# Two attention heads at a time through TensorE, in different halves of its rows and columns

## What is computed

```python
def softmax_with_sink(logits, sink):
    sink_col = jnp.broadcast_to(sink, logits.shape[:-1] + (1,))
    p = jax.nn.softmax(jnp.concatenate([logits, sink_col], axis=-1), axis=-1)
    return p[..., :-1]
...
    s_band = jnp.einsum('bkgnqd,bknsd->bkgnqs', qb, kb).astype(jnp.float32) * scale
    s_band = jnp.where(valid, s_band, NEG_INF)
    s_ctx = jnp.einsum('bkgnqd,bksd->bkgnqs', qb, kc).astype(jnp.float32) * scale
    p = softmax_with_sink(jnp.concatenate([s_band, s_ctx], axis=-1), sink_b).astype(v.dtype)
    o = (jnp.einsum('bkgnqs,bknsd->bkgnqd', p[..., :3 * BLOCK], vb)
         + jnp.einsum('bkgnqs,bksd->bkgnqd', p[..., 3 * BLOCK:], vc))
```

## Time and profile before

| | |
|---|---|
| median of three runs | 2931.18 us (2930.18 to 2934.03) |
| profiled execution | 2938.37 us, its span 2936.5 us |
| TensorE busy | 2618.6 us, 89% of the span |
| VectorE busy | 1804.7 us, 61% |
| ScalarE busy | 1053.3 us, 36% |
| chain that ended last | TensorE 50%, VectorE 15%, DMA 7%, ScalarE 6% of the span |

### The profile page before, as it was taken

One profiled execution on the slowest core, in us unless ns is written; L12 is line 12 of the kernel. 1 busy time (PEld: TensorE's weight loads), 2 busy tenths in 40 slices (PEclk: granted clock), 3 DMA queues, 4 the chain that ended last, 5 costly groups with the idle time before them and its releaser, 6 DMA issues.

```text
span 2936.5 us, 34811 instructions
## 1 busy us (share of the span) xinstructions
PE 2618.6 (89%) x13100; PEld 1942.9 (66%) x13100; DVE 1804.7 (61%) x3315; ACT 1053.3 (36%) x1930; POOL 443.0 (15%) x575
## 2 busy tenths in 40 slices
PE   6899997999997997899987999999789999698997
PEld 2788885645886996333443888887377777357776
DVE  2775786556656786234557556555578872555895
ACT  2222222223223343210332222223347862244784
POOL 1011110100001110002000433443012210100220
PEclk9899998999998998897997999999889999797999
DMA  6566662422244785110101000000159982004896
GB/s 245 168 200 201 208 190 71 167 72 72 74 164 156 250 289 165 36 63 24 36 22 36 1 1 1 1 1 1 58 199 353 339 312 79 15 8 131 303 335 220
DMA packets 115047, 386.72 MB, mean 132 GB/s; under 512 B 20160, under 2 KB 22336, under 8 KB 114624
## 3 DMA queue, kind: packets, MB, share of 16 engines
q1 hardware_dynamic: 76640, 276.33, 27.6%
q0 software_dynamic: 34848, 95.47, 10.1%
q10 hardware_dynamic: 3392, 12.70, 1.1%
HBM read 389.66 MB, written 26.21 MB: 142 GB/s over the span
## 4 chain that ended last, share of the span: by engine, by line
PE 50%; DVE 15%; DMA 7%; ACT 6%; issue 2%; POOL 1%; DVEq 0%; ACTq 0%; SPq 0%; POOLq 0%
PE ps L143 49%; DMA RG<-in_w 6%; DVE moe0wl L152 2%; DVE moe1wl L152 2%; DVE acc L160 1%; PE ps L146 1%; ACT moe0wh L149 1%; DMA AR<-in_a 1%; DVE rwMM L172 1%; ACT moe1wh L149 1%; DVE rwa L152 1%; DVE H L160 1%; ACT L149 1%; POOL rwML L152 0%; DVE X L160 0%
## 5 line engine op out<-in xcount | busy, mean ns | idle before, releaser
L143 PE MATMUL ps<-H,RG 128*128 128x256 f32 (+2 forms) x1088 | 365.8, 494 | 15.1 <-ACT H L149 15.1
L160 DVE SCALAR_TENSOR_TENSOR acc<-AR,cs,acc 128x512 f32<-128x512 f32 x420 | 296.4, 747 | 45.4 <-DMA AR<-in_a 43.3
L143 PEld LDWEIGHTS ps<-H,RG 128*128 128x128 f32 (+1 forms) x1088 | 209.2, 195 | 160.8 <-issue 135.0
L152 DVE TENSOR_TENSOR moe0wl<-RG,moe0wh 128x1024 fp32r<-128x1024 f32 x144 | 173.7, 1222 | 39.7 <-ACT moe0wh L149 36.1
L199 POOL DMA_DIRECT2D AR<-in_a x152 | 81.6, 537 | 695.2 <-DVE acc L160 534.4
L149 ACT ACTIVATE moe0wh<-RG 128x1024 fp32r<-128x1024 f32 x144 | 152.1, 1062 | 73.4 <-DMA RG<-in_w 37.3
L152 DVE TENSOR_TENSOR moe1wl<-RG,moe1wh 128x1024 fp32r<-128x1024 f32 x120 | 144.4, 1222 | 29.3 <-ACT moe1wh L149 26.6
L152 DVE TENSOR_TENSOR rwXX<-rwXX,ps 128x512 f32<-128x512 f32 x144 | 92.6, 643 | 111.2 <-PE ps L143 111.2
L149 ACT ACTIVATE f1wh<-RG 128x1024 fp32r<-128x1024 f32 x66 | 70.0, 1062 | 230.7 <-PE ps L143 230.5
L143 PE MATMUL ps<-f1hh,f1wh 128*128 128x512 f32 x352 | 142.8, 406 | 8.6 <-DVE f1hl L152 8.6
L149 ACT ACTIVATE moe1wh<-RG 128x1024 fp32r<-128x1024 f32 x120 | 126.3, 1061 | 56.3 <-DMA RG<-in_w 29.1
(11 more groups left out here) (634 smaller groups left out, 6295.1 us busy)
## 6 DMA issues: line engine op xcount, KB each, us to landing
RG<-in_w SPq DMA_DIRECT2D x525, 512.0 KB, 4.8
AR<-in_a POOLq DMA_DIRECT2D x152, 512.0 KB, 3.9
moe0back<-moe_outs ACTq DMA_DIRECT2D x4, 1024.0 KB, 8.0
CT<-in_consts ACTq DMA_DIRECT2D x1, 2546.0 KB, 18.4
X<-in_x ACTq DMA_DIRECT2D x1, 2048.0 KB, 11.5
moe_rows<-moe0ht POOLq DMA_DIRECT2D x4, 512.0 KB, 5.0
moe1back<-moe_outs ACTq DMA_DIRECT2D x2, 1024.0 KB, 5.8
X<-in_ctx ACTq DMA_DIRECT2D x1, 1024.0 KB, 7.0
```

The lines of the kernel that those rows point to most:

```text
L143: return Silent() if self.e is None else self.e.matmul(out, lhs, rhs, start=start, stop=stop, skip_group_check=True)
L152: return Silent() if self.e is None else self.e.tensor_tensor(out, a, b, op)
L160: return Silent() if self.e is None else self.e.scalar_tensor_tensor(out=out, in0=a, scalar=s, in1=b, op0=op0, op1=op1)
```

## The change

`Attention` takes pairs of heads. In each round TensorE computes the scores of both heads, one after the other into two banks, and transposes the weights of both; VectorE and ScalarE do their steps for one head and then the other. The weighted sums of a pair go into one bank, head 0 in partitions 0 to 63 and head 1 in 64 to 127, with the products of the two alternating, and one copy of 128 partitions empties it. In m1 and GQA the two heads of a pair lie in partitions 0 to 63 and 64 to 127; in MLA both lie in partitions 0 to 95. Weighing comes one round behind instead of two, the turn two instead of three. There are 2 x 4 + 3 = 11 rounds in m1 instead of 20, and 19 in MLA and in GQA instead of 36. A round takes two steps of the modulation instead of one. m1's projections stand in rounds 2 to 9, MLA's in rounds 3, 5, to 15, with ScalarE one and VectorE two rounds behind. The ring of exponentials has 6 slots (3 rounds of 2), the turned weights are kept for 2 pairs.

```diff
-    LAG, RINGS = 3, 5
-
-    def __init__(self, g, st, S, name, ada, units, scale, dv):
-        self.g, self.S, self.name, self.ada, self.units, self.scale, self.dv = g, S, name, ada, units, scale, dv
+
+    LAG, RINGS = 2, 6
+
+    def __init__(self, g, st, S, name, ada, pairs, scale, dv):
+        self.g, self.S, self.name, self.ada, self.pairs, self.scale, self.dv = g, S, name, ada, pairs, scale, dv
         self.E = g.sb(st, name + "s", [P, self.RINGS, 512])
-        self.PT = g.sb(st, name + "pt", [P, 3, 4, 256])
+        self.PT = g.sb(st, name + "pt", [P, 2, 2, 4, 256])
         self.sm = g.sb(st, name + "sm", [P, self.RINGS, 8])
-        self.n = len(units)
+        self.n = len(pairs)
 
     def ready(self):
         return [self.S.dve.at(("o", self.n - 1))]
 
     def parts(self, u):
 
-        n2 = 2 * self.n
-        return (u if u < n2 else None, u - 2 if 2 <= u < n2 + 2 else None, u - self.LAG if self.LAG <= u < n2 + self.LAG else None,
-                (u - self.LAG - 2) // 2 if u >= self.LAG + 2 and (u - self.LAG) % 2 == 0 else None)
+        inside = lambda r: r if 0 <= r < 2 * self.n else None
+        pair = u - self.LAG - 2
+        return inside(u), inside(u - 1), inside(u - self.LAG), pair // 2 if pair >= 0 and pair % 2 == 0 else None
 
     def rounds(self):
         return range(2 * self.n + self.LAG + 1)
@@ -1382,32 +1383,42 @@
                 beside(e, u)
             now, weigh, turn, pair = self.parts(u)
             if now is not None:
-                q, k, nk, vs, out, mask, sink = self.units[now // 2]
-                h = now % 2
-                ps = g.banks.take((name, "s", now))
-                for tok in g.banks.free((name, "s", now)):
-                    e.wait_ge(*tok)
-                e.matmul(ps[:, 0:nk], q[:, h * P:(h + 1) * P], k, True, True).then_inc(*p.up(("s", now)))
-            self.ada.fill_pe(e, 1)
+                qs, ks, nk, vs, out, masks, sinks = self.pairs[now // 2]
+                h, got = now % 2, []
+                for s in range(2):
+                    got.append(g.banks.take((name, "s", now, s)))
+                    for tok in g.banks.free((name, "s", now, s)):
+                        e.wait_ge(*tok)
+                for s in range(2):
+                    e.matmul(got[s][:, 0:nk], qs[s][:, h * P:(h + 1) * P], ks[s], True, True).then_inc(*p.up(("s", now, s)))
+            self.ada.fill_pe(e, 2)
             if turn is not None:
-                nk = self.units[turn // 2][2]
-                ps = g.banks.take((name, "t", turn))
-                for tok in g.banks.free((name, "t", turn)):
-                    e.wait_ge(*tok)
-                e.wait_ge(*S.dve.at(("w", turn)))
-                for j in range(nk // P):
-                    ins = e.transpose(ps[:, j * P:(j + 1) * P], self.E[:, turn % self.RINGS, j * P:(j + 1) * P], g.C("ident"))
-                ins.then_inc(*p.up(("t", turn)))
+                nk = self.pairs[turn // 2][2]
+                for s in range(2):
+                    ps = g.banks.take((name, "t", turn, s))
+                    for tok in g.banks.free((name, "t", turn, s)):
+                        e.wait_ge(*tok)
+                    e.wait_ge(*S.dve.at(("w", turn, s)))
+                    for j in range(nk // P):
+                        ins = e.transpose(ps[:, j * P:(j + 1) * P], self.slot(turn, s)[:, j * P:(j + 1) * P], g.C("ident"))
+                    ins.then_inc(*p.up(("t", turn, s)))
             if pair is not None:
-                q, k, nk, vs, out, mask, sink = self.units[pair]
+                qs, ks, nk, vs, out, masks, sinks = self.pairs[pair]
                 ps = g.banks.take((name, "o", pair))
                 for tok in g.banks.free((name, "o", pair)):
                     e.wait_ge(*tok)
-                e.wait_ge(*S.act.at(("t", 2 * pair + 1)))
-                b = out.base_partition()
+                e.wait_ge(*S.act.at(("t", 2 * pair + 1, 1)))
                 for j in range(nk // P):
-                    ins = e.matmul(ps[b:b + self.dv, 0:256], vs[j], self.PT[:, pair % 3, j, :], j == 0, j == nk // P - 1)
+                    for s in range(2):
+                        ins = e.matmul(ps[s * self.dv:(s + 1) * self.dv, 0:256], vs[s][j], self.PT[:, pair % 2, s, j, :], j == 0,
+                                       j == nk // P - 1)
                 ins.then_inc(*p.up(("o", pair)))
+
+    def ring(self, r, s):
+        return (2 * r + s) % self.RINGS
+
+    def slot(self, r, s):
+        return self.E[:, self.ring(r, s), :]
 
...
-            if now is not None:
-                q, k, nk, vs, out, mask, sink = self.units[now // 2]
-                m, s = self.sm[:, now % self.RINGS, :], self.E[:, now % self.RINGS, 0:nk]
-                e.wait_ge(*S.dve.at(("m", now)))
-                if sink is not None:
-                    e.activation(m[:, 2:3], sink, ACT.Exp, bias=m[:, 1:2]).then_inc(*a.up())
-                src, sc = (s, 1.0) if mask is not None else (g.banks.of((name, "s", now))[:, 0:nk], self.scale)
-                e.activation(s, src, ACT.Exp, bias=m[:, 1:2], scale=sc, accum_out=m[:, 3:4]).then_inc(*a.up(("e", now)))
-                if mask is None:
-                    g.banks.done((name, "s", now), a.now())
-            if turn is not None:
-                nk, tp, h = self.units[turn // 2][2], turn // 2, turn % 2
-                e.wait_ge(*S.pe.at(("t", turn)))
-                if tp >= 3:
-                    e.wait_ge(*S.pe.at(("o", tp - 3)))
-                e.activation(self.PT[:, tp % 3, 0:nk // P, h * P:(h + 1) * P],
-                             g.banks.of((name, "t", turn))[:, 0:nk].rearrange("p (j n) -> p j n", n=P),
-                             ACT.Copy).then_inc(*a.up(("t", turn)))
-                g.banks.done((name, "t", turn), a.now())
+            for i in range(2) if now is not None else ():
+                qs, ks, nk, vs, out, masks, sinks = self.pairs[now // 2]
+                m, s = self.sm[:, self.ring(now, i), :], self.slot(now, i)[:, 0:nk]
+                e.wait_ge(*S.dve.at(("m", now, i)))
+                if sinks is not None:
+                    e.activation(m[:, 2:3], sinks[i], ACT.Exp, bias=m[:, 1:2]).then_inc(*a.up())
+                src, sc = (s, 1.0) if masks is not None else (g.banks.of((name, "s", now, i))[:, 0:nk], self.scale)
+                e.activation(s, src, ACT.Exp, bias=m[:, 1:2], scale=sc, accum_out=m[:, 3:4]).then_inc(*a.up(("e", now, i)))
+                if masks is None:
+                    g.banks.done((name, "s", now, i), a.now())
+            for i in range(2) if turn is not None else ():
+                nk, tp, h = self.pairs[turn // 2][2], turn // 2, turn % 2
+                e.wait_ge(*S.pe.at(("t", turn, i)))
+                if tp >= 2:
+                    e.wait_ge(*S.pe.at(("o", tp - 2)))
+                e.activation(self.PT[:, tp % 2, i, 0:nk // P, h * P:(h + 1) * P],
+                             g.banks.of((name, "t", turn, i))[:, 0:nk].rearrange("p (j n) -> p j n", n=P),
+                             ACT.Copy).then_inc(*a.up(("t", turn, i)))
+                g.banks.done((name, "t", turn, i), a.now())
 
...
-            if weigh is not None:
-                q, k, nk, vs, out, mask, sink = self.units[weigh // 2]
-                m, s = self.sm[:, weigh % self.RINGS, :], self.E[:, weigh % self.RINGS, 0:nk]
-                e.wait_ge(*S.act.at(("e", weigh)))
-                if sink is not None:
+            for i in range(2) if weigh is not None else ():
+                qs, ks, nk, vs, out, masks, sinks = self.pairs[weigh // 2]
+                m, s = self.sm[:, self.ring(weigh, i), :], self.slot(weigh, i)[:, 0:nk]
+                e.wait_ge(*S.act.at(("e", weigh, i)))
+                if sinks is not None:
                     e.tensor_tensor(m[:, 3:4], m[:, 3:4], m[:, 2:3], ADD).then_inc(*v.up())
                     e.wait_ge(*v.now())
                 e.reciprocal(m[:, 4:5], m[:, 3:4]).then_inc(*v.up())
                 e.wait_ge(*v.now())
-                e.tensor_scalar(s, s, m[:, 4:5], None, MUL).then_inc(*v.up(("w", weigh)))
-            if now is not None:
-                q, k, nk, vs, out, mask, sink = self.units[now // 2]
-                m, s = self.sm[:, now % self.RINGS, :], self.E[:, now % self.RINGS, 0:nk]
-                ps = g.banks.of((name, "s", now))
-                e.wait_ge(*S.pe.at(("s", now)))
-                if now >= self.RINGS:
-                    e.wait_ge(*S.pe.at(("t", now - self.RINGS)))
...
-            self.ada.fill_dve(e, 1)
+                    e.tensor_scalar(m[:, 1:2], m[:, 0:1], -sc, None, MUL).then_inc(*v.up(("m", now, i)))
+            self.ada.fill_dve(e, 2)
             if pair is not None:
-                out = self.units[pair][4]
-                b = out.base_partition()
                 e.wait_ge(*S.pe.at(("o", pair)))
-                e.tensor_copy(out, g.banks.of((name, "o", pair))[b:b + self.dv, 0:256]).then_inc(*v.up(("o", pair)))
```

(49 more changed lines are left out.)

27 lines of the change are left out of this document (17 added, 10 removed).

## The result

Four runs of the changed kernel gave a median of **2849.77 us** (2841.62 to 2854.80), against 2932.61 for the kernel before beside them: ratio 0.971, 95% interval 0.9687 to 0.9732. It is faster by 83 us; I had forecast 65. The profiled execution took 2853.85 us, its span 2852.1, 84.4 less than the span before.

A forecast was written before the change was run, and what follows sets the result against it. TensorE was taken to bound all three attentions. Savings of 25 us in GQA, 22 in m1 and 18 in MLA, 65 in all, led from the median 2931.18 to 2866 us; 80% range 2850 to 2888.

The forecast's parts named there:

- parts 1 and 2: TensorE: two heads' scores in different rows, and sums in different columns, run together; GQA pair 6.03 us instead of 10.26.
- rival (d): Sums overlap and scores do not: m1 loses 6.9 us, GQA 5 (TensorE 7.7 a pair); 2878 us; chance 0.05.
- rival (a): The array's halves do not run together: GQA pair 9.4 us on TensorE; time 2909 us; chance 0.07.
- The circle: GQA: waits from sum through VectorE and ScalarE to the next sum set 7.16 us a pair; GQA 25 us less.
- part 4: m1: 16.9 us less work, 5 us less waiting, nothing counted for half clock; 22 us less (14 to 29).
- m1 89: Sign that the forecast is right: m1's stage near 89 us in the profile after.
- MLA's sign, 97: Sign that the forecast is right: MLA's stage near 97 us in the profile after.
- part 5: MLA: sums halve, 11.5 us, and half of the idle time goes, 6.5; 18 us less (11 to 24).
- What follows each attention: Stages after each attention start from the same state and wait on nothing the change moves: 0 us.
- The shorter lag: GQA: weighing one round behind makes VectorE wait for ScalarE, so a pair takes 7.16 us, not 6.03; price 1.1 a pair.
- (b): Strict order within a pair: 0.43 us more per pair of scores, 0.21 per sum; 2872 us; chance 0.06.
- (c): Slower clock, as TensorE stands idle in GQA: about 2950 us with two thirds at half clock; chance 0.03.

The follow-up runs named there:

- maxima first: The changed kernel with VectorE doing this round's maxima before the weighings of the round before: 2841.7 us, ratio 0.9701.
- the lag alone: The changed kernel with weighing two rounds behind and the turn three, as before, and 8 slots for exponentials: 2832.2 us, ratio 0.9666.
- the copies first: The changed kernel with turn three rounds behind, weighing one, maxima ahead of weighings, and ScalarE's copies ahead of its exponentials: 2824.3 us, ratio 0.9626.
- the executions listed above: Profiled executions: four with m1 as before (13.6, 10.2, 6.8, 6.8 us at half clock), six with the changed kernel's m1 rounds (3.4, 3.4, 0, 0, 0, 0).
- the run without pairs: The kernel before with m1's projections moved by one round, to odd rounds 1 to 15: 2925.3 us, ratio 0.9966.
- the run with the same rows: The changed kernel with the second head's scores in m1 and GQA computed from the first head's rows: 2868.6 us, ratio 0.9791.

## Why the prediction was off

The number, 2866, was 16 us too high, and the time lies 0.2 us below my range. The mechanism of the pairs was right. What failed are two terms that I put at nothing: the steps of the modulation, which I took for the same work in both (5.9 us), and m1's half clock, of which I counted "none" (5.1 us in the two profiled executions). Point by point, by these two:

- **Rows and columns overlap** (parts 1 and 2): right. Four score passes take 1.06 from start to start (2518.00 to 2519.06), as worked out; a sum of a pair 1.88, for 1.87. TensorE's 6.03 us for a pair came out at 6.04 once nothing else bound it. Without the overlap of rows, rival (d), m1 took 6.5 us more (6.9 said) and TensorE 7.75 a pair in GQA (7.7 said), but GQA as a whole 9.9 and not 5. Without that of columns a sum took 3.57 from start to the next start (3.58 in rival (a)).
- **The circle** (part 3): right as to its links but one, and 0.06 us too long (7.16 for 7.10). I had the second maximum in it, 0.91 us; measured, ScalarE's two exponentials follow one another (0.78 and 0.78). That the two came close is luck in the parts, not in the mechanism: with the weighings out of it (maxima first) the period fell, with the lag alone, which leaves every link in it, it stayed at 7.10, and with the copies first it fell to TensorE's own. GQA's own 2 us more than forecast come from those 0.06 a pair and from the last pair, which drained in 5.3 us instead of 7.16.
- **m1** (part 4): a failed step. The work was right, 16.9 forecast and 16.8 shown. The waits fell by 6.4 where I took 5, although ScalarE's copy of a projection, which I said "holds up nobody", held up TensorE's transposes for 1.9. The clock was counted at nothing, "worth up to 6.5": 13.6 us at half before and 3.4 after, so 10.2 us less at half, 5.1 us of TensorE's time. 16.8 + 6.4 + 5.1 = 28.3 of 29.1. Over the executions listed above (9.4 us at half on average before, 1.1 after) the clock is worth some 4 us, an estimate. In the run without pairs, waits and half clock both went with nothing halved; the run with the same rows had half clock without the waits, so that one causes the other is not shown. The "m1 89" that I named as a sign came true by two errors: the gain 7 us too small, and a stage of before that lacked a projection of 6.9. MLA's sign, 97, failed by the same window: measured 101.95, with the projection of 7.1 in it.
- **MLA** (part 5): 2.4 too small. Idle time fell by 5.8 (6.5 forecast), TensorE's busy time by 14.6 (11.5 forecast). Of those 3.1 us, 1.7 are a stretch of 3.4 us that ran at half clock before and has no like in after. Most of the rest is, by an estimate, what a change of shape costs around a sum, which the 11.5 leave out: four transposes ahead of a sum take 0.58 (1388.84 to 1389.42 in after), others 0.44 (1439.38 to 1439.82 in before), and there are 8 sums fewer, 8 x 0.14 = 1.1 us.
- **What follows each attention** ("wait on nothing the change moves"): the other failed step, wrong by 7.8 us, 5.9 of them shown. I had written of the modulation sums that they are "the same work in both", and had not asked how many rounds take them: 11 rounds of two are 22 steps, 20 rounds of one are 20, and the two that were missing stood exposed 500 us later.
- **The shorter lag** (part 3): I priced it in GQA's circle alone. The longer lag leaves that circle at 7.10 and still saves 13 to 17 us, in MLA, in m1 and at GQA's ends. In MLA I wrote that half of the idle time goes, and did not ask what keeps the rest: of the 7.8 us left, 4.2 are waits for ScalarE's copies, and with the longer lag 0.2.
- **Rivals.** (b), strict order of the program, is refuted for these passes: two heads' passes in turns, or in blocks of four, cost no extra slot. The Trainium skill's rule in "TensorE: Matmul & The Clock Gate" (Part 3: Packing small matmuls — row/col tiling), that matmuls begin and end strictly in program order, does not hold in this trace: with eight passes of head 0 in front, head 1's first (by the two series of starts) began beside the fifth, ahead of three that stand before it. (c), the clock, went the other way: the mean granted clock of the profiled executions rose from 0.933 to 0.940, although TensorE stands idle 0.98 us in each 7.10 of GQA.

So of the 19.4 us between 65 and 84.4, 5.9 lay in the modulation, 7.1 in m1 (5.1 of it clock), 2.4 in MLA, 2.1 in GQA and 1.9 elsewhere. My range came from bounds of the three stages alone; it had no term for what lies outside them, although the change altered how many steps a stage takes of a shared queue.
